# Shift and scale columns as row sums on VectorE from transposed weights, with the first two projection blocks taken K tile by K tile

## The reference, cut to what matters

```python
def modulation(c, w, b):
    return jnp.split(jax.nn.silu(c) @ w + b, 3, axis=-1)

def sandwich(x, mod, g_pre, g_post, fn):
    shift, scale, gate = mod
    h = rms_norm(x, g_pre) * (1.0 + scale[:, None]) + shift[:, None]
    return x + gate[:, None] * rms_norm(fn(h), g_post)

# first_block, per layer (ada_w is (DEPTH, 2, 1024, 3072))
x = sandwich(x, modulation(c, ada_w[layer, 0], ada_b[layer, 0]), norm_pre[layer, 0], norm_post[layer, 0], mixer)
x = sandwich(x, modulation(c, ada_w[layer, 1], ada_b[layer, 1]), norm_pre[layer, 1], norm_post[layer, 1], ffn)

# mixer of layer 0
u, qr, fr, vr, gr = jnp.split(h @ hyb_w_in[j], split_at, axis=-1)      # 1024 -> 2560
y = jnp.concatenate([pool_mixer(u, ...), hgrn2_mixer(qr, fr, vr, gr, ...)], axis=-1)
return y @ hyb_w_out[j]
```

## Time and profile before

| | us |
|---|---|
| median of 3 runs | 1270.07 |
| lowest, highest | 1269.45, 1270.67 |
| profiled execution | 1269.97 |
| its span (first to last instruction) | 1268.2 |

### The profile page before, as it was taken

One profiled execution on the slowest core, in us unless ns is written; L12 is line 12 of the kernel. 1 busy time (PEld: TensorE's weight loads), 2 busy tenths in 40 slices (PEclk: granted clock), 3 DMA queues, 4 the chain that ended last, 5 costly groups with the idle time before them and its releaser, 6 DMA issues.

```text
span 1268.2 us, 20841 instructions
## 1 busy us (share of the span) xinstructions
PE 1248.5 (98%) x8024; PEld 1133.6 (89%) x8024; DVE 933.9 (74%) x1222; ACT 718.2 (57%) x1069; POOL 50.8 (4%) x76
## 2 busy tenths in 40 slices
PE   8999999999999999999999999999999999999999
PEld 6998899999999778999989989888888888888888
DVE  6889988886899658666676695676666677666665
ACT  3676754444744557444467764665555667655554
POOL 1101000000111000000001000000000000000000
PEclk8999999999999999999999999999999999999999
DMA  9986989996799734666556544356565542366650
GB/s 348 372 297 208 339 290 325 334 327 205 244 361 370 230 67 153 206 203 200 199 166 211 162 150 155 132 198 200 200 202 202 190 163 95 122 220 204 202 166 34
DMA packets 147248, 274.41 MB, mean 216 GB/s; under 512 B 4759, under 2 KB 85679, under 8 KB 147048
## 3 DMA queue, kind: packets, MB, share of 16 engines
q1 hardware_dynamic: 132320, 220.21, 51.5%
q0 software_dynamic: 13616, 50.94, 11.9%
q10 hardware_dynamic: 1240, 2.26, 0.5%
HBM read 272.30 MB, written 1.10 MB: 216 GB/s over the span
## 4 chain that ended last, share of the span: by engine, by line
PE 82%; DVE 8%; DMA 4%; ACT 3%; issue 2%; ACTq 0%; POOL 0%; DVEq 0%; POOLq 0%
PE ps L2229 80%; DMA ada_ring<-in_ada_w 4%; DVE wlo L1299 2%; DVE acc_a L1316 2%; ACT whi L542 1%; PE ps L2682 1%; DMA voh<-in_voh 1%; ACT xn L603 0%; PE ps L2416 0%; PE ps L2399 0%; DVE rs L1949 0%; ACT h L659 0%; DVE prob L1906 0%; ACT hboth L654 0%; PE ps L2976 0%
## 5 line engine op out<-in xcount | busy, mean ns | idle before, releaser
L1299 DVE TENSOR_TENSOR wlo<-raw,whi 128x1024 fp32r<-128x1024 f32 x400 | 483.5, 1222 | 222.8 <-ACT whi L542 222.0
L542 ACT CAST whi<-raw 128x1024 fp32r<-128x1024 f32 x400 | 416.6, 1048 | 404.0 <-PE ps L2229 389.6
L2229 PE MATMUL ps<-hboth,whi 128*128 128x256 f32 (+1 forms) x2720 | 605.2, 311 | 1.0 <-DVE hboth L1529 0.5
L2229 PE MATMUL ps<-hboth,wlo 128*128 128x256 f32 x1792 | 491.6, 274 | 0.7 <-DVE hboth L1524 0.4
L2229 PEld LDWEIGHTS ps<-hboth,whi 128*128 128x128 f32 x2720 | 447.2, 191 | 30.1 <-issue 6.2
L2229 PEld LDWEIGHTS ps<-hboth,wlo 128*128 128x128 f32 x1792 | 343.9, 192 | 3.1 <-issue 0.6
L2229 PE MATMUL ps<-whi,hidhi 128*128 128x512 f32 x434 | 164.5, 379 | 0.0
L2229 PE MATMUL ps<-wlo,hidhi 128*128 128x512 f32 x434 | 164.1, 378 | 0.0
L2229 PE MATMUL ps<-whi,hidlo 128*128 128x512 f32 x434 | 164.1, 378 | 0.0
L2229 PE MATMUL ps<-whi,hboth 128*128 128x512 f32 (+1 forms) x512 | 155.8, 375 | 3.0 <-DVE wlo L1299 0.9
L2229 PEld LDWEIGHTS ps<-whi,hboth 128*128 128x128 f32 x512 | 95.5, 190 | 18.5 <-issue 5.1
(11 more groups left out here) (259 smaller groups left out, 1118.6 us busy)
## 6 DMA issues: line engine op xcount, KB each, us to landing
raw<-in_ffn_w_in SPq DMA_DIRECT2D x44, 1024.0 KB, 7.2
ada_ring<-in_ada_w POOLq DMA_DIRECT2D x40, 1024.0 KB, 7.9
raw<-in_w_mlp_up SPq DMA_DIRECT2D x32, 1024.0 KB, 5.4
raw<-in_w_mlp_down SPq DMA_DIRECT2D x32, 1024.0 KB, 4.9
raw<-in_ffn_w_out SPq DMA_DIRECT2D x22, 1024.0 KB, 5.1
raw<-in_att_w_qkv SPq DMA_DIRECT2D x18, 1024.0 KB, 7.3
raw<-in_w_in_even SPq DMA_DIRECT2D x18, 1024.0 KB, 5.1
raw<-in_hyb_w_in SPq DMA_DIRECT2D x10, 1024.0 KB, 11.2
```

The lines of the kernel that those rows point to most:

```text
L542: A.copy(whi[:, H % 4, :], raw[:, slot(n), h * HALF:(h + 1) * HALF]).then_inc(s["hi_ready"], 1)
L1299: V.tensor_tensor(wlo[:, H % 4, :], raw[:, slot(n), h * HALF:(h + 1) * HALF], whi[:, H % 4, :].bitcast(F32), ALU.subtract).then_inc(s["lo_ ...
L2229: return pe.matmul(out, lhsT, rhs, start=first, stop=last, skip_group_check=True)
```

## The change

Shift and scale weights are also laid out transposed in DRAM (`ada_t`: one row per output column, 1024 numbers of k), and `c` as a row. `silu(c)` stands on every partition in `scrow`. A column of 128 shifts or scales is then one VectorE instruction, `weighted_row`: 128x1024 weights times `scrow`, added along the row, the bias as start value. Nothing is left for TensorE: `sum_cols`, `add_cols`, `ada_cols` and `mod_cols` are gone. A gate piece is now one 128x1024 row block (`gate_items`) instead of two of 128x512. `ada_ring` has four slots of 0.5 MB instead of two of 1 MB.

```diff
@@ VectorE
-            def ada_item(acc, b, n, k, it=0, bias=None):
...
+            def weighted_row(row, j, c):
+                name, dst, k = ("b_scale", scol, c - KD) if c >= KD else ("b_shift", shcol, c)
+                return V.tensor_tensor_reduce(out=row, in0=row, in1=scrow[:, :], scale=1.0, scalar=col(name, 8 * j + k),
+                                              op0=ALU.mult, op1=ALU.add, accum_out=dst[:, j, k:k + 1])
...
+            def first_chunk(k):
+                at = ADA_AT[k]
+                dve.wait_ge(raw_in[at % RAW], 16 * (at // RAW + 1))
+                weighted_row(raw[:, at % RAW, 0:D], 0, k)
+                weighted_row(raw[:, at % RAW, D:], 0, KD + k).then_inc(s["ada_used"], 1)
+                dve.wait_ge(s["ada_used"], k + 1)
+                V.tensor_tensor(scol[:, 0, k:k + 1], scol[:, 0, k:k + 1], col("g_pre", k), ALU.mult) \
                     .then_inc(s["mod_ready"], 1)
...
-            for a in range(4):
-                ada_first(a)
             mean_x(0, 0)
+            scaled_x(0)
             mean_x(0, 1)
-            for a in range(4, ADA_FIRST):
-                ada_first(a)
-            mod_cols(0, 0)
-            split(0)
-            pre(0)
+            for k in range(KD):
+                first_chunk(k)
+                split(k)
+                first_low(k)
@@ ScalarE
+            act.dma_start(scrow[:, :], row_of(t["c_row"], D)).then_inc(s["cols_in"], 16)
             act.dma_start(ident[:, :], t["ident"]).then_inc(s["const_in"], 16)
...
+            for k in range(KD):
+                split(k)
+                if k == 0:
+                    act.wait_ge(s["turned"], KD)
+                act.wait_ge(s["mod_ready"], k + 1)
...
             act.wait_ge(s["vec_dil_c"], 4)
             act.dma_start(t["vec_dil"].rearrange("g h n -> h g n"),
@@ TensorE
-            sum_cols(acc_a, 0, 0)
-            turn(3, 4)
+            turn(3, 14)
...
+            warm_ones(12)
+            pe.wait_ge(s["xn_ready"], 1)
+            for k in range(KD):
+                pe.transpose(turned_ps(0, k)[:, 0:P], xn1[:, 0, k * P:(k + 1) * P], ident[:, :])
+            pe.wait_ge(s["diag_ready"], 1)
...
             pe.wait_ge(s["vec_dil_c"], 4)
-            turn(0)
...
+            for k in range(KD):
+                first_tile(k)
             pe.wait_ge(s["proj_free"], 1)
             pe.wait_ge(s["band_in"], 48)
```

More of the change, by code:

```diff
@@ L285, in xn_of, with ring @@
             return (xn1, h321) if j < 4 else (xn2, h322)
+        def ring(n):
+            return HYB_AT[n] if 0 <= n < len(HYB_AT) else n + ADA_FIRST
         def slot(n):
[L289 removed]
+            return ring(n) % RAW
         def in_count(n):
[L293 to L295 removed]
+            return 16 * (ring(n) // RAW + 1 + sum(a <= ring(n) and a % RAW == slot(n) for a in HYB_AT))
+        ada_flat = ada_ring[:, :, :].rearrange("p a b -> p (a b)")
         pt2, yd = ada_flat[:, 0:20 * P], ada_flat[:, 20 * P:20 * P + S]
@@ L1544, in swiglu, with items, body @@
                 H0, G = 2 * n, NG1 * call
-                def body(g, it=0, before=range(2), after=range(2, 6), ada=None, bias=None):
+                def items(g, a, b):
+                    if not modulations or g >= 8:
+                        return
+                    r = range(4 * (g % 2) + a, 4 * (g % 2) + b)
+                    if g < 2:
+                        gate_items(1, acc_b, r)
+                    elif g < 6:
+                        col_items(2, [8 * (g // 2 - 1) + k for k in r])
+                    else:
+                        gate_items(2, acc_a, r)
+                def body(g, it=0, before=range(2), after=range(2, 6)):
                     dve.wait_ge(s["gate_ready"], G + g + 1 + 2 * it)
```

371 lines of the change are left out of this document (178 added, 193 removed).

## The result

| | before | after |
|---|---|---|
| median of 5 runs, us | 1270.07 | 1275.59 |
| lowest, highest | 1269.31, 1270.67 | 1274.75, 1277.25 |
| profiled execution (span) | 1269.97 (1268.2) | 1276.46 (1274.7) |

The ratio is 1.0039, with a 95% interval of 1.0026 to 1.0052 (the two medians alone would give 1.0043): the change makes the kernel 0.4% slower. Between the two profiled executions lie 6.5 us of span. Behind 500 us the shift of a product against its counterpart stays within 0.02 us of 6.49, so all of it is made by the end of the third turn.

The account below looks back on a forecast made before the run. After the first slices, with DMA nine tenths busy over much of the first 350 us, TensorE's product sequence decides. 4.5 + 1.5 - 2.0 - 1.4 = 2.6 us later than 1269.97: 1272.6, range 1267.4 to 1278.5.

Parts of the forecast that it names:

- First operands: Kernel start up to tile 0: `voh` lands at 12.6 us, fillers take 4.2 us, tile 0 is ready at 25.8.
- One K tile: VectorE's work per K tile at the start: row sum 1.2 us, 4.05 us a tile, TensorE finishes tile 7 at 56.7.
- the dear sum: Rival, K tiles: a row sum costs double, 2.3 us; seven tiles cost 16 us more, about 1288; chance 0.04.
- low clock: Rival, K tiles: TensorE runs them at the low clock, 5.2 us a tile, and sets their pace; 1274.1; chance 0.08.
- What is late next: Tables behind the K tiles: store lands in 2.0 us, tables take 7.9, pooling products start 4.5 us later.
- The clock: TensorE idle from 56.7 to 64.4 before the pooling products; the clock falls, costing 1.5 us.
- The rounds: Hybrid mixer's rounds: TensorE, being late, loses its waits for VectorE and wins back 2.0 us.
- it is just not the limit: Rounds: VectorE starts some 2 us later, reaches level 7 about 3 us later, and does not hold TensorE.
- The turns: Between sublayers, column sums and a gate product go: 0.6, 0.4 and 0.4 us won, 1.4 in sum.
- The early start: Rival: `voh` not held up, tables quick, pooling products start before about 59.5 us; 1267.4; chance 0.16.
- the sum's case: The main forecast, all terms together: 2.6 us later, 1272.6, own range 1269.8 to 1275.0; chance 0.52.
- the tables come late in full company: Rival, start: three tables take 12.6 us beside other queues, `band_in` at 69.1, 4.7 us more; 1277.3; chance 0.20.

Follow-up runs that it names:

- The warm start: Changed kernel with bias stores before the K tiles, tables behind K tile 2, 50 fillers before the bias products, tile 1's row sums earlier: 1264.65 us, ratio 0.9959.
- The fillers' experiment: Changed kernel with 36 filler products between the last K tile and the wait for the tables: 1275.63 us, ratio 1.0043.
- The short sums: Changed kernel with bias stores and tables before the K tiles, and six row sums of rounds 1 to 6 over 32 elements: 1265.23 us, ratio 0.9956.
- the first experiment: Changed kernel with ScalarE's two stores of the bias vectors issued before its K tiles, tables left in place: 1281.81 us, ratio 1.0091.
- the two warm starts: The warm start (1264.65 us), and the same with block 2's first half ahead of the pooling products and 23 first-turn fillers instead of 12 (1264.62 us).

## Why the prediction was right or wrong

The direction was the likeliest by the chances (slower 0.48), and 1275.59 lies in the range; the size, 2.6 us, was less than half of the 5.5 measured (6.5 in the profiled execution). Three costs were too small (the tables, the clock, the first turn), one gain too large (the rounds), and one gain was missing, which hid part of this: without the 1.5 us won in the projections the time would have been about 1277. Step by step:

- **First operands: right but for the fillers.** `voh` at 13.0 (12.6 forecast). The 24 filler records took 5.3 us, not 4.2: I assumed that the clock would rise under them as it had from 15.55 on in the earlier trace rows, and it rose only at their end. Tile 0 was ready at 27.4, not 25.8. 1.0 us of it reached the stores, whose issue runs ahead of ScalarE's last operation. The warm start shows what this step was worth: I treated the low clock as given.
- **One K tile: right.** Pitch 4.11 (4.05). The row sum at one pass, the dear sum refuted, no low clock.
- **What is late next: the mechanism right, one term short.** The store landed 3.85 us after its issue, not 2.0. I had taken the row of the output stores, which have the queues to themselves. Issue to last landing of the tables was 7.83 (7.9). But it is a soft number: 7.8, 8.1, 9.9, 11.4 and 15.0 us over the five kernels that issue the same tables behind the K tiles, in one execution each. With the tiles' delay the pooling products are 7.1 us late (4.5).
- **The clock: 2.5 us, not 1.5.** I halved 3 us; the clock was low from 61.7 to 71.9 us, so the pooling products, from 66.96 to 72.73, ran at the low level for all but their last 0.8 us. The fillers' experiment shows the price.
- **The rounds: -0.75, not -2.0.** The waits of the earlier trace rows at levels 2 and 3 went, 1.4 us with what is not shown there, while the one at level 8 stayed (0.75 of 0.85 us). I had counted it as a wait for VectorE, and its row does not say so: it ends with "issue", and the changed kernel's names ScalarE. And VectorE's row sums cost 0.84 again at levels 5 and 6. The step that failed is "it is just not the limit". I counted the difference of 0.45 us a round and forgot that VectorE had no idle time in the rounds before either, so that the differences add up. The short sums show it: 1.7 us.
- **The turns: the second and third right** (0.41 and 0.49, forecast 0.4 each). The first gave 0.7 us back on VectorE (last product to transposes 5.1 instead of 5.8; forecast 0.6) and lost 1.4 behind the transposes, of which 0.3 came back in the next products; 1.1 of the 1.4 is the clock's (9.44 us from the last product of `hyb_out` to the first of the SwiGLU, 8.3 in the kernels where it stayed full). I had not asked what keeps TensorE busy once the column products are gone: they had been its filler.
- **Not in the sum: 1.5 us won in the attention's projections**, from two waits of TensorE that I had not looked for, since the sum had VectorE's work behind the first turn "not later".

Against the 2.6 us of the sum the errors are +2.6 at the pooling products, +1.0 by the clock, +1.2 in the rounds, +0.7 at the first turn (with 0.2 won in `hyb_out`), -1.5 in the projections and -0.1 at the third turn: 6.5. The early start (0.16) failed at its condition: `voh` was held up. The case that came true is the sum's case with larger terms, not "the tables come late in full company", whose wait of 12.6 us for the tables only the first experiment reached (15.0).

## What to carry to other kernels

Before an engine or a queue is relieved, list what it will trigger sooner, and which transfers, of its own and of other queues, that will then run beside; a load that needs nothing belongs into the stretch where the DMA share is zero, even if memory has to be rearranged for it. An operation that looks like waste on TensorE may be what keeps its clock: where it is removed ahead of a wait, put fillers in its place. When steps are hoisted on one engine, check the release order of every in-order queue that they feed.

## What the runs showed of the hardware

- A transfer of 256 KB took 7.0, 7.2, 8.0, 10.5 and 14.2 us from issue to landing behind the K tiles of five kernels (the changed one and four that differ from it in one edit), one execution each. While the longest was on its way, the other queues issued eight transfers of 0.5 or 1 MB; during the shortest, three. Two stores of 52 KB together took 3.9 to 4.8 us at a full DMA share, where the earlier trace rows has 2.0 for 256 KB in a quiet one.
- The same idle stretch of 2.04 to 2.05 us ahead of the first turn's transposes, behind the same 24 filler records, ended at full clock in four kernels and at the low one in six. In and behind the K tiles of the two warm starts, idle stretches of 2.22, 2.82 and 2.87 us kept the full clock, and behind those of 2.05, 2.07, 2.21 and 2.62 us it was low. All waits of 1.25 us kept it; all of 3.3 us and more lost it. So between 2.0 and 2.9 us the length of the stretch alone does not decide; what does is open here.
- Products of 33 rows by 8 columns took 5.6 us for eight records begun at the low clock and 2.9 at the full one; begun low, they did not bring it up (in the changed kernel they ran from 13.0 to 18.6 us, and the clock rose at 24.1).
